# Moving the large SBUF buffers of a hybrid decoder step by 128 bytes

## The chip, the core and the metric

The kernel runs on one core of a Trainium2 chip, and all its work is in one launch. The metric is the device time in microseconds (us). TensorE (PE) multiplies matrices, and PEld is the part of it that loads weights; VectorE (DVE), ScalarE (ACT) and GpSimd (POOL) do elementwise work; SyncE (SP) issues DMAs. SBUF is the working memory that all of them read, 128 partitions side by side; every buffer begins at the same byte in each partition. TensorE writes to PSUM.

## The reference, cut to what matters

One inference step of a two-layer decoder on 576 tokens: 512 of a prompt and 64 of eight decoding sequences. The model is 1024 wide, and everything is float32.

```
for layer l in 0, 1:
    x += 0.5 * FFN_a(RMSNorm(x))      # silu(x @ w_gate) * (x @ w_up) @ w_down, inner width 2816
    x += Mixer_l(RMSNorm(x))          # layer 0: mLSTM matrix memory; layer 1: gated linear attention
    x += 0.5 * FFN_b(RMSNorm(x))
out = RMSNorm(x)
```

Outputs are the normed activations of all tokens, the new mixer states, normalisers, running maxima and the last convolution rows.

## The kernel before

Activations stay in SBUF with features on the partitions: `x` is 128 partitions x 8 tiles x 576 tokens. Each product of two float32 matrices is made from three products of `float32r` parts (`split_product`): high weight by high activation, high weight by low activation, low weight by high activation. So there are two buffers for each operand: `xn_hi` and `xn_lo` (normed activations), `w_hi` and `w_lo` (weights), `h_hi` and `h_lo` (the FFN's inner tiles), `th_hi` and `th_lo` (sums of activation tiles, for the blocks that `seven_pair` makes with seven products in place of eight).

A weight block is loaded by DMA into one of four slots of `raw`, 4096 bytes in each partition. ScalarE rounds it into `w_hi` (line 1185), VectorE writes what is left into `w_lo` (line 1753), and TensorE then multiplies with it. SyncE issues the load of a block once the block four places earlier has been split (lines 350 and 357), so that loads run ahead of the products.

The program goes through phases: for each FFN, three groups of a gate-and-up phase (G) and a down phase (D); for each mixer, QK, MIX and OUT. The first G of every FFN, the mixers and the very last D are written out in a straight line; other G and D phases are hardware loops. The plain products all stand on line 479, in `split_product`: tokens are cut in two halves of 288, and two matmuls with the same weights and the two halves follow one another (columns 0 to 287, then 288 to 575), into two PSUM banks. Those of `seven_pair` stand on line 536; line 753 makes the value tiles, with activations as weights. Lines 608, 784 and 787 are small products inside the mixers. Other names below: `gate_hi` and `gate_lo` are the few weight columns of the mixers' gates, read in slices that begin 144 bytes apart in mixer 0; `state` is the running prompt state of a mixer; `scratch` is ten tiles of 576 tokens for intermediate values; `n_in` is the incoming normaliser of the decoding sequences, 32 numbers (128 bytes) in each partition, read twice for each head in the mLSTM mixer (lines 2335 and 2339).

Buffers are laid out in the order of their declarations, each behind the one before. Where a name is closed again (`inner.close()`), the next declaration takes its place.

Of the kernel before, what the change touches and what calls it, by code (L numbers as in the profile page):

```python
# [7 lines left out]
SEQ, DEC_BATCH, DEC_SEQ = 512, 8, 8  # L8
N_HEADS, DK, DV = 4, 128, 256
# [5 lines left out]
P = 128  # L15
# [87 lines left out]
def program(nc, io):  # L103
# [4 lines left out]
    with ctx:  # L108
        def sb(name, shape, dt=f32):
            return ctx.enter_context(nc.sbuf_tensor(name, shape, dt))  # L110
# [2 lines left out]
            return ctx.enter_context(nc.semaphore(name))  # L113


        x = sb("x", [P, KT_X, TOK])

        inner = ExitStack()
# [33 lines left out]
        cols = sb("cols", [P, TT, 2 * N_HEADS])  # L152
        w_a2 = sb("w_a2", [GATE_RANK, N_HEADS * DK])
        b_a = sb("b_a", [P, N_HEADS])
        n_in = sb("n_in", [P, N_HEADS, DEC_BATCH])
        n_out = sb("n_out", [P, N_HEADS, DEC_BATCH + 1])
        n_state = sb("n_state", [P, N_CH])
        neg_b_a = sb("neg_b_a", [P, N_HEADS])
# [2568 lines left out]
```

How the kernel before makes its waits and increments, by code:

```python
            def load_mix(pair, mixer, first):  # L345
                for blk in range(2):
                    s = 2 * (pair % 2) + blk
                    sp.wait_ge(lo_done, 2 * pair + blk - 3)
                    sp.dma_start(raw[:, s, :], io["w_mix"][32 * mixer + first + blk, :, :]).then_inc(raw_full[s], 16)
# [1 line left out]
            def load(ph, i, s, first=False):  # L352
                n = 2 * ph["base"] + 4 * i + s
                if not first:
                    sp.wait_ge(lo_done, n - 3)
                sp.dma_start(raw[:, s, 0:ph["k"] * P],
                             block_source(ph, i, s).rearrange("o p n -> p (o n)")).then_inc(raw_full[s], 16)
# [1 line left out]
            def state_load(mixer, h):  # L360
                src, u = io["state_c"] if mixer == 0 else io["state_g"], N_HEADS * mixer + h
                if u:
                    sp.wait_ge(state_out, 32 * u)
                sp.dma_start(state_s[:, :, :], src[:, h, :, :].rearrange("b k v -> k b v")).then_inc(state_in, 16)
# [1 line left out]
            def state_store(mixer, h):  # L368
                dst_s, dst_p = (io["c_s"], io["c_p"]) if mixer == 0 else (io["s_s"], io["s_p"])
                sp.wait_ge(state_ready, N_HEADS * mixer + h + 1)
                sp.dma_start(dst_s[:, h, :, :].rearrange("b k v -> k b v"), state_s[:, :, :]).then_inc(state_out, 16)
                sp.dma_start(dst_p[h, :, :], state[:, N_CH - 1, :]).then_inc(state_out, 16)
# [196 lines left out]
            def token_sums(norm):  # L570
                pe.wait_ge(ssq_done, 4 * (norm + 1))
                if norm == 0:
```

## Time and profile before

| what | value |
|---|---|
| median of 3 runs | 2197.02 us (2196.39 to 2197.16) |
| profiled execution, first to last instruction | 2198.8 us |
| TensorE busy | 2160.5 us, 98% |
| VectorE busy | 1555.5 us, 71% |
| ScalarE busy | 951.1 us, 43% |
| GpSimd busy | 45.7 us, 2% |
| mean granted TensorE clock | 0.994 |
| moved by DMA | 201.58 MB, 92 GB/s |

The profiled execution is one run taken by the hardware profiler; its span is 1.8 us above the median of the runs that were only timed. The busy time of TensorE counts the stretch in which at least one matmul is under way. Matmuls overlap, so that "98% busy" says only that it had no gaps; how fast it goes is read from how many matmuls start in a stretch.

### The profile page before, as it was taken

The page shows a single profiled execution, that of the slowest core. Times are in us where ns is not written, and L with a number is a line of the kernel's source. Part 1 is how long each engine was busy: PE and PEld are TensorE (multiplying, and loading weights), DVE is VectorE, ACT ScalarE, POOL GpSimd, SP SyncE. Part 2 cuts the span into 40 slices and gives each one's busy share as a digit, 9 for nine tenths or more (in the row PEclk, how much of TensorE's full clock was granted, in tenths as well). Part 3 has the DMA queues.
Part 4 walks back from the last instruction along what each step waited for, and adds up shares of the span by engine and source line. Part 5 has one row for each costly group of instructions (what it writes and reads, how often), then busy time and mean ns, then how long its engine had stood idle before and what let it go on. Part 6 is the DMA issues. An engine that isn't in the chain of part 4 may idle for free.

```text
span 2198.8 us, 40702 instructions
## 1 busy us (share of the span) xinstructions
PE 2160.5 (98%) x16360; PEld 2137.4 (97%) x16360; DVE 1555.5 (71%) x2379; ACT 951.1 (43%) x1495; POOL 45.7 (2%) x50
## 2 busy tenths in 40 slices
PE   7999999999999999999999999999999999999997
PEld 7999999999999999999999999999999899999997
DVE  6898657685555798848679984863776457988485
ACT  5435435454433444515445452544322434445252
POOL 0000000001100000000000000000011100000000
PEclk9999999999999999999999999999999999999999
DMA  5222322224332232222323232232122222223222
GB/s 186 68 88 95 115 67 86 96 82 137 99 118 85 68 102 82 95 87 89 104 70 94 86 96 96 82 101 94 44 96 84 97 77 84 90 87 104 77 86 73
DMA packets 72578, 201.58 MB, mean 92 GB/s; under 512 B 7268, under 2 KB 26980, under 8 KB 72448
## 3 DMA queue, kind: packets, MB, share of 16 engines
q1 hardware_dynamic: 72448, 199.80, 28.1%
q8 instruction: 88, 1.44, 0.3%
q14 instruction: 42, 0.34, 0.1%
HBM read 187.82 MB, written 11.95 MB: 91 GB/s over the span
## 4 chain that ended last, share of the span: by engine, by line
PE 91%; DVE 5%; ACT 2%; issue 1%; DMA 0%; POOL 0%; SPq 0%; DVEq 0%; POOLq 0%
PE ps L479 48%; PE ps L536 32%; PE ps L753 4%; PE ps L608 1%; DVE w_lo L1768 1%; PE ps L784 1%; PE ps L773 1%; PE ps L787 0%; DVE w_lo L1753 0%; PE ps L803 0%; PE ps L617 0%; PE ps L796 0%; PE ps L631 0%; PE ps L797 0%; DMA x<-in_x 0%
## 5 line engine op out<-in xcount | busy, mean ns | idle before, releaser
L479 PE MATMUL ps<-h_lo,w_hi 128*128 128x288 f32 x1616 | 347.0, 294 | 4.1 <-DVE h_hi L2267 4.1
L479 PE MATMUL ps<-h_hi,w_hi 128*128 128x288 f32 x1616 | 346.5, 294 | 0.7 <-DVE w_lo L1753 0.7
L536 PE MATMUL ps<-th_hi,w_hi 128*128 128x288 f32 x1088 | 320.2, 294 | 2.4 <-ACT scratch L1219 2.4
L536 PE MATMUL ps<-th_lo,w_hi 128*128 128x288 f32 x1088 | 320.9, 295 | 0.0
L536 PE MATMUL ps<-th_hi,w_lo 128*128 128x288 f32 x1088 | 319.8, 294 | 0.0
L479 PE MATMUL ps<-h_hi,w_lo 128*128 128x288 f32 x1360 | 290.2, 292 | 0.0
L479 PE MATMUL ps<-xn_hi,w_hi 128*128 128x288 f32 x1152 | 257.2, 300 | 11.6 <-DVE w_lo L1753 8.9
L479 PEld LDWEIGHTS ps<-h_lo,w_hi 128*128 128x128 f32 x1616 | 259.9, 188 | 4.8 <-DVE h_hi L2267 4.5
L479 PEld LDWEIGHTS ps<-h_hi,w_hi 128*128 128x128 f32 x1616 | 259.9, 188 | 1.0 <-DVE w_lo L1753 0.9
L1753 DVE TENSOR_TENSOR w_lo<-raw,w_hi 128x1024 fp32r<-128x1024 f32 x196 | 232.2, 1221 | 36.9 <-ACT w_hi L1185 35.1
L479 PE MATMUL ps<-xn_hi,w_lo 128*128 128x288 f32 x1152 | 251.9, 296 | 0.0
L479 PE MATMUL ps<-xn_lo,w_hi 128*128 128x288 f32 x1152 | 251.7, 296 | 0.0
L1768 DVE TENSOR_TENSOR w_lo<-scratch,w_hi 128x512 fp32r<-128x512 f32 x272 | 181.8, 690 | 84.8 <-ACT w_hi L1200 84.4
L1185 ACT ACTIVATE w_hi<-raw 128x1024 fp32r<-128x1024 f32 x196 | 195.8, 1047 | 105.2 <-PE ps L479 80.5
L536 PE MATMUL ps<-xn_hi,w_lo 128*128 128x288 f32 x816 | 240.4, 295 | 0.0
L536 PE MATMUL ps<-xn_hi,w_hi 128*128 128x288 f32 x816 | 239.9, 294 | 0.0
L536 PE MATMUL ps<-xn_lo,w_hi 128*128 128x288 f32 x816 | 239.9, 294 | 0.0
L479 PEld LDWEIGHTS ps<-h_hi,w_lo 128*128 128x128 f32 x1360 | 217.5, 187 | 0.0
L536 PEld LDWEIGHTS ps<-th_hi,w_hi 128*128 128x128 f32 x1088 | 204.8, 188 | 3.7 <-issue 3.2
L479 PEld LDWEIGHTS ps<-xn_hi,w_hi 128*128 128x128 f32 x1152 | 187.7, 190 | 19.9 <-issue 17.5
L2019 DVE SCALAR_TENSOR_TENSOR x<-ps,x 128x1152 f32<-128x1152 f32 x52 | 70.5, 1356 | 191.9 <-PE ps L479 191.9
L536 PEld LDWEIGHTS ps<-th_hi,w_lo 128*128 128x128 f32 x1088 | 204.4, 188 | 0.0
(288 smaller groups left out, 4119.7 us busy)
## 6 DMA issues: line engine op xcount, KB each, us to landing
raw<-in_w_gate SPq DMA_DIRECT2D x88, 512.0 KB, 3.4
raw<-in_w_up SPq DMA_DIRECT2D x88, 512.0 KB, 4.2
raw<-in_w_down SPq DMA_DIRECT2D x64, 512.0 KB, 3.6
raw<-in_w_mix SPq DMA_DIRECT2D x64, 512.0 KB, 4.2
raw<-in_w_down SPq DMA_DIRECT2D x32, 384.0 KB, 3.2
state_s<-in_state_c SPq DMA_DIRECT2D x4, 1024.0 KB, 7.5
out_c_s<-state_s SPq DMA_DIRECT2D x4, 1024.0 KB, 4.6
state_s<-in_state_g SPq DMA_DIRECT2D x4, 1024.0 KB, 6.1
```

What stands on the lines that cost most here:

```text
L479: ins = nc.tensor.matmul(o, a, b[:, c] if c is not None else b, start=first and j == 0, stop=last and j == 2)
L536: ins = nc.tensor.matmul(ps[:, bank, FIRST], left, b_, start=first and k == 0 and j == 0, stop=k == KT_X // 2 - 1 and j == 2, skip_group_c ...
L608: ins = nc.tensor.matmul(ps[:, bank, c * P:(c + 1) * P], left[:, ts], right[:, ts], start=True, stop=True)
L753: ins = nc.tensor.matmul(out, a[:, k, xs], b[:, 2 * half:2 * half + 2, ws], start=k == 0 and j == 0, stop=k == KT_X - 1 and j == 2)
L773: ins = nc.tensor.matmul(ps[:, 4 + c // 2, (c % 2) * DV:(c % 2 + 1) * DV], k_tok[:, c, :], v_tok[:, 1 + c, h * DV:(h + 1) * DV], start=Tru ...
L784: ins = nc.tensor.matmul(out, v_tok[:, 1 + c, vs], att(mixer, h)[:, c * P:(c + 1) * P], start=True, stop=c == 0)
L1185: nc.scalar.activation(w_hi[:, slot, :], raw[:, slot, :], ACT.Copy).then_inc(hi_done, 1)
L1753: V.tensor_tensor(w_lo[:, slot, :], raw[:, slot, :], w_hi[:, slot, :].bitcast(f32), ALU.subtract).then_inc(lo_done, 1)
L1768: return V.tensor_tensor(by_tile(unit(w_lo, half, u)), src, by_tile(unit(w_hi, half, u)).bitcast(f32), ALU.subtract)
L2019: ins = V.scalar_tensor_tensor(xs, ps[:, b:b + 4, 0:HALF_TOK], scale, xs, ALU.mult, ALU.add)
```

## The change

The declaration of `n_in` moves from behind `b_a` to the front, ahead of `x`.

```diff
@@ -113,6 +113,7 @@
             return ctx.enter_context(nc.semaphore(name))


+        n_in = sb("n_in", [P, N_HEADS, DEC_BATCH])
         x = sb("x", [P, KT_X, TOK])

         inner = ExitStack()
@@ -152,7 +153,6 @@
         cols = sb("cols", [P, TT, 2 * N_HEADS])
         w_a2 = sb("w_a2", [GATE_RANK, N_HEADS * DK])
         b_a = sb("b_a", [P, N_HEADS])
-        n_in = sb("n_in", [P, N_HEADS, DEC_BATCH])
         n_out = sb("n_out", [P, N_HEADS, DEC_BATCH + 1])
```

On every engine the same instructions stand in the same order as before; only addresses in them differ. The first byte of each buffer in a partition, as the two programs are built:

| buffer | size | before | after | before mod 256 | after mod 256 |
|---|---|---|---|---|---|
| `n_in` | 128 | 207264 | 1152 | 160 | 128 |
| `x` | 18432 | 1152 | 1280 | 128 | 0 |
| `xn_hi` | 18432 | 19584 | 19712 | 128 | 0 |
| `xn_lo` | 18432 | 38016 | 38144 | 128 | 0 |
| `raw` | 16384 | 56448 | 56576 | 128 | 0 |
| `w_hi` | 16384 | 72832 | 72960 | 128 | 0 |
| `w_lo` | 16384 | 89216 | 89344 | 128 | 0 |
| `h_hi` (also `qt`, `kt`) | 18432 | 105600 | 105728 | 128 | 0 |
| `h_lo` (also `og`) | 18432 | 124032 | 124160 | 128 | 0 |
| `th_hi` (also `v_tok`) | 18432 | 142464 | 142592 | 128 | 0 |
| `scratch` | 23040 | 162944 | 163072 | 128 | 0 |
| `cst` | 4384 | 188608 | 188736 | 192 | 64 |
| `gate_hi` | 2112 | 196064 | 196192 | 224 | 96 |
| `gate_lo` | 2112 | 198176 | 198304 | 32 | 160 |
| `th_lo` (also `state`, `state_s`) | 18432 | 207808 | 207808 | 192 | 192 |

All that is declared between `x` and `b_a` moves by 128 bytes; `n_out` and what follows it stay.

## Rows read from the trace of the kernel before

**Rows 1.** The page: busy time, granted clock in 40 slices, and the chain by line.
```profile
PE 2160.5 (98%) x16360; PEld 2137.4 (97%) x16360; DVE 1555.5 (71%) x2379; ACT 951.1 (43%) x1495; POOL 45.7 (2%) x50
...
PEclk9999999999999999999999999999999999999999
...
PE ps L479 48%; PE ps L536 32%; PE ps L753 4%; PE ps L608 1%; DVE w_lo L1768 1%; PE ps L784 1%; PE ps L773 1%; PE ps L787 0%; DVE w_lo L1753 0%; PE ps L803 0%; PE ps L617 0%; PE ps L796 0%; PE ps L631 0%; PE ps L797 0%; DMA x<-in_x 0%
```

**Rows 2.** Waits of TensorE, longest in total first: us, times, longest.
```profile
PE ps L479 <- DVE w_lo L1753: 9.5, 2, 8.9
PE ps L479 <- DVE h_hi L2267: 4.1, 2, 2.1
PE ps L1118 <- DVE scratch L2588: 3.7, 1, 3.7
PE ps L536 <- ACT scratch L1219: 2.4, 4, 0.7
```

**Rows 3.** Busy time by stretch, instructions as (x), clock, DMA; G, G, D, QK, OUT, seven.
```profile
48.00:80.00 32.00, 32.00 (x243) 32.00 (x242) 21.23 (x32) 10.63 (x14) 0.00 (x0) 1.00 0.21 67
728.00:760.00 32.00, 32.00 (x248) 32.00 (x247) 22.55 (x32) 11.96 (x15) 0.00 (x0) 1.00 0.20 66
800.00:832.00 32.00, 32.00 (x248) 32.00 (x247) 30.94 (x33) 12.98 (x13) 0.00 (x0) 1.00 0.23 78
432.00:464.00 32.00, 32.00 (x242) 32.00 (x242) 29.36 (x64) 19.88 (x31) 0.24 (x2) 1.00 0.22 67
664.00:696.00 32.00, 32.00 (x242) 32.00 (x241) 15.44 (x14) 10.16 (x12) 0.00 (x0) 1.00 0.30 96
200.00:232.00 32.00, 32.00 (x244) 32.00 (x244) 27.77 (x50) 18.89 (x39) 0.00 (x0) 1.00 0.25 83
```

**Rows 4.** Groups of matmuls by line and form: count, busy us, mean ns.
```profile
L479 PE MATMUL ps<-h_lo,w_hi 128*128 128x288 f32 x1616 | 347.0, 294 | 4.1 <-DVE h_hi L2267 4.1
L536 PE MATMUL ps<-th_lo,w_hi 128*128 128x288 f32 x1088 | 320.9, 295 | 0.0
L536 PE MATMUL ps<-th_hi,w_lo 128*128 128x288 f32 x1088 | 319.8, 294 | 0.0
```

**Rows 5.** TensorE in order of time, from the first gate matmul to the one after.
```profile
413.81 0.43 PE L479 MATMUL ps<-xn_hi,gate_hi 128*128 128x288 f32 x2
...
420.19 0.30 PE L479 MATMUL ps<-xn_hi,w_hi 128*128 128x288 f32 x1
```

**Rows 6.** TensorE in order of time in the mLSTM mixer: start us, us.
```profile
500.70 0.61 PE L784 MATMUL ps<-scratch,v_tok 128*128 128x128 f32 x4
501.15 0.39 PE L787 MATMUL ps<-qt,state 128*128 128x128 f32 x2
501.37 0.39 PE L784 MATMUL ps<-scratch,v_tok 128*128 128x128 f32 x2
```

**Rows 7.** All engines in order of time, start of the program.
```profile
8.86 0.82 PE L479 MATMUL ps<-xn_hi,w_hi 128*128 128x288 f32 x2 [8.86 <-DVE w_lo L1753]
```

**Rows 8.** Waits of ScalarE for DMAs.
```profile
ACT xn_hi L1274 <- DMA x<-in_x: 3.2, 2, 2.9
ACT w_hi L1185 <- DMA raw<-in_w_up: 0.2, 1, 0.2
ACT gate_hi L1694 <- DMA n_in<-in_n_in: 0.2, 1, 0.2
```

**Rows 9.** Weight loads: KB each and median us to landing; then SyncE's waits.
```profile
raw<-in_w_gate SPq DMA_DIRECT2D x88, 512.0 KB, 3.4
raw<-in_w_up SPq DMA_DIRECT2D x88, 512.0 KB, 4.2
...
SPq L357 <- DVE w_lo L1768: 817.5, 136, 18.2
```

**Rows 10.** Busy time by stretch: start, and the tail behind the last FFN matmul.
```profile
0.00:9.00 9.00, 0.14 (x1) 0.18 (x2) 2.94 (x4) 4.93 (x6) 0.52 (x5) 1.00 0.76 283
...
2184.60:2198.80 14.20, 1.33 (x2) 0.50 (x2) 8.77 (x16) 1.13 (x2) 0.00 (x0) 0.63 0.41 142
```

## The prediction

> **What bounds the kernel now.** I read the page first, then the waits of TensorE, then stretches of 32 us inside single phases. The page has TensorE busy for 2160.5 of 2198.8 us at a granted clock of nine tenths or more in all 40 slices (full speed, 2.4 GHz), and the chain that ended last is TensorE's, 48% on line 479 and 32% on line 536 [rows 1]. Its waits are few: the largest are 9.5 us for a weight split, nearly all at the start, 4.1, 3.7 and 2.4 us [rows 2]. So the time is, to within some 40 us, the number of matmuls times the pace at which they start.
>
> That pace is the one thing that a new address could move by much, so I read it closely. A matmul of 288 columns shows a duration of 294 ns [rows 4], but they overlap; a window of 32 us counts every one that touches it, so the pace is (32.00 + 0.29) us over the count. It is 132.9 ns in the G phase at 48 us and 130.2 ns in the G phase at 728 us; the D loop at 800 us has 130.2, the QK phase at 432 us and the OUT phase at 664 us have 133.4, and the seven-product loop at 200 us has 132.3 [rows 3]. The two G stretches are the same lines with the same buffers at the same addresses, and still differ by 2.7 ns. The pace of line 479 thus has two levels, and which one holds is not fixed by the addresses alone.
>
> **The change part by part.** No instruction is added, removed or moved. All costs are therefore differences in how long the same instruction takes, or the same transfer.
>
> *Moving operands of the matmuls.* An activation tile of `xn_*`, `h_*` or `th_*` is read in halves of 1152 bytes = 9 x 128. The 16 halves of a buffer therefore begin at all 16 multiples of 128 within 2048 bytes, each once. A shift by 128 only permutes that set. Whatever a start costs by its place within 256, 512, 1024 or 2048 bytes, the sum over a buffer is the same: 0 us. The one operand that does not move is `th_lo`, at 192 mod 256 beside `th_hi` at 128: its halves start at odd multiples of 64, the others' at multiples of 128. Its matmuls show 295 ns, those of `th_hi` 294 [rows 4], and the loop that uses both goes at 132.3 ns, between the two paces of the loops that never touch it [rows 3]. The place of that operand costs nothing that I can see.
>
> *Weights.* This is the only real novelty. Weight tiles are 512 bytes, so all of `w_hi` and `w_lo` begin at 128 mod 512 before and at 256 mod 512 after. Nearest rows: the gate weights, whose slices begin 144 bytes apart from 224 mod 256 (every place in steps of 16 bytes, 0 mod 256 among them). Their 48 matmuls take 420.19 - 413.81 = 6.38 us, 132.9 ns each, which is not above the 133.4 of ordinary weights in the same phase [rows 5, 3]. Short matmuls of 128 columns, where the weight load must show, start every 0.11 us with weights of `v_tok` (128 mod 256: 0.45 us for four) as with weights of `state` (192 mod 256: 0.22 us for two) [rows 6]. The three kinds agree within 0.5 ns for the long form. I take 0. The ends: 0.5 ns either way on the 15,200 long matmuls of lines 479, 536 and 753 (16360 in all less about 1,100 short ones) is 7.6 us either way; that is the resolution of these rows, not a sign of an effect.
>
> *Relative places.* A weight load runs under the previous matmul, so two reads of SBUF meet. Between weights and moving operands all distances stay as they were, except to `th_lo` and `state`. Cost 0, by the same rows.
>
> *VectorE and ScalarE.* They have slack: VectorE is busy 71%, ScalarE 43% [rows 1]. If all their instructions took 1% more, only where TensorE waits for them would it show: 1% of the roughly 20 us of waits in [rows 2] and of the 14.2 us tail, where VectorE is busy 8.77 us [rows 10]: 0.3 us. I take 0, ends -0.3 and +0.3.
>
> *DMAs.* Loads of weights land 3.4 to 4.2 us after issue, while SyncE has waited 817.5 us in total for slots to come free [rows 9]: the queue, not the transfer, sets when they arrive, and ScalarE waited for a weight load once, 0.2 us [rows 8]. Even a load that takes a tenth longer is covered. Only the start is bare: the first matmul begins at 8.86 us [rows 7], and before it ScalarE waits 3.2 us in total for `x` [rows 8] while the DMA engines are 76% busy [rows 10]. A transfer that gets 5% shorter or longer there is worth 5% of 9 us, 0.45 us. I take -0.1.
>
> Here the Trainium skill has a rule that speaks for a gain ("DMA: Bandwidth & Descriptors", section "How a descriptor splits into AXI transactions"): a transaction must start at a multiple of 256 bytes, and a descriptor that doesn't start there also pays for the bytes below it. If it holds for the SBUF side of a load, a row of 4096 bytes at 128 mod 256 costs 132 beats of 32 bytes before and 128 after, an estimate of 3% from that page. By it the start would gain about 0.3 us and the rest nothing, since loads are hidden; no row here shows a transfer at 0 mod 256 to compare.
>
> *`n_in` itself.* It is loaded last of the constants, one transfer of 16 KB, and ScalarE waits 0.2 us once for that group [rows 8]. VectorE reads it in eight short instructions in the mixer. 0 us.
>
> The sum: 0 + 0 + 0 + 0 - 0.1 + 0 = -0.1 us on a span of 2198.8, so 2198.7 in a profiled execution. The profiled span is 1.8 us above the timed median, so against the median of 2197.02 the forecast is 2196.9, which I give as 2197.0. What can be told from no change here is about 0.2%, 4.4 us: everything in the sum is far inside it.
>
> **The rivals.**
>
> *A, faster: the pace of the straight-line phases locks at the lower level.* The straight-line matmuls of line 479 that now run at 133.3 ns are at most 480 in the first G phase, 1536 in the two mixers and 768 in the two OUT phases, 2784. If the new addresses brought them all to 130.0, the gain is 2784 x 3.3 ns = 9.2 us: 2187.8. For it: the same code with the same operands runs at either pace [rows 3], so something slight decides, and it may be the history of the run, in which addresses could play a part. Against it: three timed runs lie within 0.8 us, so that the timing noise of a run doesn't flip the levels, and all distances between operands stay.
>
> *B, slower: the loops lock at the upper level.* The D loops now run at 130.2 ns [rows 3]. They issue 22 tiles x 8 blocks x 6 matmuls for each of 4 FFNs, less the last D phase of 288, so 3936. At 133.3 ns they cost 3936 x 3.3 ns = 13.0 us more: 2210. If only a third of them flipped, it would be +4.3 us, the point from which the verdict is slower. The place where it would decide is the weight load of line 479 at its new start, 256 mod 512, under a moving read. For it: the same as for A, and no steady loop of before has had weights there. Against it: the gate weights, at 16-byte steps, are no slower than the rest [rows 5].
>
> *C: the address matters in the weights of every long matmul by one more or one less step of access.* Bounded above at 0.5 ns either way, 7.6 us: 2189.4 or 2204.6. Against it stands that three kinds of weights agree. The Trainium skill ("SBUF — State Buffer", section "Specifications (TRN2)") counts lines of 16 bytes; every start of a large buffer is a multiple of 16 before and after, so by that page the sum stays 0.
>
> *D: the change is only in the DMAs.* That gives at most 0.45 us, within the forecast's own range.
>
> **How the numbers follow.** No measurable change (the sum, with D): 0.77. A, or the faster half of C: 0.12. B, or the slower half of C: 0.11. The likeliest one's own range is 2195.3 to 2198.7: the spread of the runs before (0.8 us) doubled, plus 0.8 us for DMAs and side engines. The two sides together hold 0.23, more than may be left out, so the range reaches half of A (2192.4) and the lower third of B (2201.3): 2192.0 to 2201.0. The chances of faster by over 0.2%, within it, and slower by over it are 0.12, 0.77 and 0.11.
>
> **What would show it.** If I am right, a window of 32 us holds 242 or 243 matmuls at 48, 432 and 664 us, 248 at 728 and 800 us, and 244 at 200 us, as now; the waits of TensorE stay near 9.5, 4.1, 3.7 and 2.4 us; the first matmul starts at 8.4 to 9.3 us. A shows as 248 in the windows of QK and OUT, B as 242 in the D loops, C as a count that is shifted in all windows at once. The landing time of weight loads tells of the DMA rule: 3.4 us would fall to 3.3 with no effect on TensorE. The prediction is wrong if the time leaves 2192.6 to 2201.4.

## The result, and the profile after

The changed kernel takes 2214.16 us (median of 4 runs, 2211.35 to 2216.96) against 2197.09 us (4 runs): a ratio of 1.0075, 95% interval 1.0061 to 1.0089. It is 17 us slower. The forecast was 2197.0 us, no measurable change. The interval leaves room for a difference of 13.4 to 19.6 us. The profiled executions last 2198.8 us before and 2210.4 us after.

The page of the changed kernel, its busy time, answers to [rows 1]:

```profile
span 2210.4 us, 40702 instructions
...
PE 2171.0 (98%) x16360; PEld 2148.1 (97%) x16360; DVE 1554.1 (70%) x2379; ACT 949.3 (43%) x1495; POOL 47.5 (2%) x50
```

The same instructions; VectorE and ScalarE are as busy as before to within 2 us, and TensorE is busy 10.5 us longer. TensorE's waits answer to [rows 2] and have hardly moved:

```profile
PE ps L479 <- DVE w_lo L1753: 10.1, 2, 9.4
PE ps L479 <- DVE h_hi L2267: 4.1, 2, 2.1
PE ps L1118 <- DVE scratch L2588: 3.7, 1, 3.7
PE ps L536 <- ACT scratch L1219: 2.3, 4, 0.7
```

So it is the pace of the matmuls. The changed kernel by stretch, in the order of [rows 3] (G, G, D, QK, OUT, seven-product loop), the columns as there; after the second PE column stands the number of matmuls:

```profile
48.00:80.00 32.00, 32.00 (x242) 32.00 (x241) 22.75 (x33) 11.03 (x14) 0.00 (x0) 1.00 0.20 67
728.00:760.00 32.00, 32.00 (x249) 32.00 (x248) 21.70 (x29) 13.12 (x17) 0.00 (x0) 1.00 0.24 82
800.00:832.00 32.00, 32.00 (x242) 32.00 (x241) 30.39 (x34) 14.09 (x14) 0.00 (x0) 1.00 0.28 93
432.00:464.00 32.00, 32.00 (x242) 32.00 (x241) 30.73 (x63) 20.15 (x30) 0.23 (x2) 1.00 0.20 67
664.00:696.00 32.00, 32.00 (x242) 32.00 (x241) 16.85 (x16) 12.19 (x14) 0.00 (x0) 1.00 0.25 84
200.00:232.00 32.00, 32.00 (x243) 32.00 (x243) 27.60 (x49) 18.52 (x38) 0.00 (x0) 1.00 0.24 85
```

Five of the six are as before, to one or two matmuls. The D loop at 800 us has 242 where it had 248: (32.00 + 0.29) / 242 = 133.4 ns a matmul, in place of 130.2. It is no exception: the windows of 32 us at 120, 264, 936, 1056, 1200 and 1904 us hold 242 or 243 each, where before they held 248 or 249. The window of 80 us in a seven-product loop is long enough to show the smaller step there. The kernel before, then the changed one:

```profile
170.00:250.00 80.00, 80.00 (x607) 80.00 (x607) 68.21 (x120) 45.09 (x93) 0.00 (x0) 1.00 0.30 97
```

```profile
170.00:250.00 80.00, 80.00 (x604) 80.00 (x603) 68.19 (x121) 45.11 (x93) 0.00 (x0) 1.00 0.28 94
```

That is 80.29 us over 607, 132.3 ns, against 132.9. By kind of operand, the groups of the changed kernel that answer to [rows 4] (count, busy us, mean ns):

```profile
L479 PE MATMUL ps<-h_lo,w_hi 128*128 128x288 f32 x1616 | 350.7, 296 | 4.1 <-DVE h_hi L2267 4.1
L536 PE MATMUL ps<-th_hi,w_hi 128*128 128x288 f32 x1088 | 324.1, 298 | 2.3 <-ACT scratch L1219 2.3
L536 PE MATMUL ps<-th_lo,w_hi 128*128 128x288 f32 x1088 | 322.3, 296 | 0.0
```

The `th` matmuls have grown; those of `th_hi` with `w_hi` took 320.2 us at a mean of 294 ns before. The `xn` matmuls of the same line stay at 294 ns. From one start to the next on line 536 the `th` ones now take 133.3 ns and the `xn` ones 132.3, before 132.1 and 132.3 (starts in the trace, averaged by operand; how the places where the operand changes are counted moves them by 0.1).

**The account.** By the starts in the trace all 11 D loops run at 130.0 ns before and at 133.3 after: 3936 matmuls x 3.33 ns = 13.1 us. The `th` matmuls: 3264 x 1.2 ns = 3.9 us. Three straight-line stretches that stand directly behind a D loop have slowed with it, 0.6 us in all. The clearest is a G phase of 96 matmuls, from 130.0 to 133.3 ns, before and then after:

```profile
1090.00:1101.00 11.00, 11.00 (x87) 11.00 (x86) 8.56 (x12) 7.39 (x9) 0.00 (x0) 1.00 0.34 114
```

```profile
1096.00:1107.00 11.00, 11.00 (x85) 11.00 (x84) 8.58 (x11) 6.98 (x9) 0.00 (x0) 1.00 0.31 103
```

Together 17.6 us, beside a timed difference of 17.1 that is known to 3 us either way. The profiled executions differ by only 11.6 us, since they did not have the same clock. Stretches around the places where the kernel before was profiled with TensorE's clock at half (1.2 GHz in place of 2.4) for a moment, before and then at the same places of the changed kernel, the last two of which come 10 or 11 us later:

```profile
40.00:44.00 4.00, 3.19 (x15) 3.23 (x16) 3.84 (x5) 1.08 (x2) 0.00 (x0) 0.66 0.54 155
652.00:662.00 10.00, 7.94 (x49) 7.74 (x48) 5.59 (x11) 1.41 (x3) 0.00 (x0) 0.83 0.41 133
1632.00:1642.00 10.00, 7.79 (x53) 7.62 (x52) 9.09 (x16) 3.70 (x5) 3.36 (x4) 0.83 0.00 0
1745.00:1755.00 10.00, 7.94 (x50) 7.74 (x49) 5.85 (x10) 1.24 (x2) 0.00 (x0) 0.83 0.43 151
```

```profile
40.00:44.00 4.00, 2.65 (x20) 2.69 (x21) 3.82 (x5) 1.62 (x2) 0.00 (x0) 1.00 0.37 123
652.00:662.00 10.00, 7.94 (x62) 7.74 (x61) 6.45 (x12) 2.29 (x3) 0.00 (x0) 1.00 0.24 84
1643.00:1653.00 10.00, 7.80 (x65) 7.57 (x64) 9.10 (x19) 4.74 (x6) 5.10 (x4) 1.00 0.00 0
1755.00:1765.00 10.00, 7.94 (x61) 7.73 (x60) 7.06 (x12) 2.68 (x4) 0.00 (x0) 1.00 0.40 135
```

A mean clock of 0.83 over 10 us is 3.4 us at half speed, a loss of 1.7 us; 0.66 over 4 us, with 0.91 in the next 4, is the same again. In three of these stretches TensorE had been idle for 2 us at the edge of a phase (busy 7.94 or 7.79 of 10 us), and ahead of the one at 41 us for 1.9 us. The changed kernel has the same idle times (busy 7.94, 7.80 and 7.94) and kept its full clock, so the idle time alone does not decide. The profile before has these four and one at 475 us, the profile after only the last: 4 x 1.7 = 6.8 us. 17.6 - 6.8 = 10.8 us, and the first matmul starts 0.56 us later (9.42 us, against [rows 7]); that leaves 0.2 us. The four timed runs of the changed kernel differ by 5.6 us, and their mean granted clocks go with their times: 0.997 and 0.996 in the two of 2211 and 2212 us, 0.995 and 0.994 in those of 2216 and 2217.

### The profile page after: what moved, and what is told of

It is laid out like the page before. It is cut to its first block, busy times and chain, and to the rows that moved or that the text cites. A ratio compares the mean times of both kernels' runs of the same rounds, so it can differ in the third digit from the quotient of the medians.

```text
span 2210.4 us, 40702 instructions
## 1 busy us (share of the span) xinstructions
PE 2171.0 (98%) x16360; PEld 2148.1 (97%) x16360; DVE 1554.1 (70%) x2379; ACT 949.3 (43%) x1495; POOL 47.5 (2%) x50
## 4 chain that ended last, share of the span: by engine, by line
PE 91%; DVE 5%; ACT 2%; issue 1%; DMA 0%; POOL 0%; SPq 0%; DVEq 0%; POOLq 0%
PE ps L479 48%; PE ps L536 32%; PE ps L753 4%; PE ps L608 1%; DVE w_lo L1768 1%; PE ps L784 1%; PE ps L773 1%; PE ps L787 0%; DVE w_lo L1753 0%; PE ps L803 0%; PE ps L617 0%; DMA x<-in_x 0%; PE ps L631 0%; PE ps L796 0%; PE ps L797 0%
## 5 line engine op out<-in xcount | busy, mean ns | idle before, releaser
L479 PE MATMUL ps<-h_hi,w_lo 128*128 128x288 f32 x1360 | 295.1, 296 | 0.0
```

The costliest lines, as they stand in the source:

```text
L479: ins = nc.tensor.matmul(o, a, b[:, c] if c is not None else b, start=first and j == 0, stop=last and j == 2)
```

## The experiments

All of them keep every instruction of the kernel before, except where it says that a matmul is added. The changes are places in memory. Unless a ratio is given, a time is of one execution, beside one of the kernel before. Those of the kernel before took 2194.1 to 2200.9 us, so a difference of a few us in one pair says little, and the paces decide. In each fence the rows are windows with the columns of [rows 3]: 170 us is in a seven-product loop, 264 and 800 us are in D loops, 728 us in a G phase. Before, they held 607, 249, 248 and 248 matmuls.

**1. The 128 bytes ahead of `h_hi`.** Weights, `x` and `xn` stay.

```diff
-        n_in = sb("n_in", ...)            # behind b_a
+        n_in = sb("n_in", ...)            # ahead of h_hi
```

> The 128 bytes stand ahead of h_hi: weights, raw, x and xn stay where they were before; h_hi, h_lo, th_hi, scratch and all behind them begin 128 bytes later. If the start of the weight tiles sets the pace of the D loops (theory 1), they stay at 130.0 ns a matmul, 248 in the window of 32 us at 800 us, and the time at 2197 us or, with the 0.7 ns more in the seven-product loops, up to 2201. If the start of the moving tiles h sets it (theory 2), 242 in that window and about 2212. If the history at the entry of a loop sets it (theory 3), either pace, unlike the place of any buffer.

2216.56 us, beside 2199.39. Its windows at 170 and 800 us:

```profile
170.00:250.00 80.00, 80.00 (x605) 80.00 (x604) 68.25 (x121) 45.06 (x93) 0.00 (x0) 1.00 0.29 93
800.00:832.00 32.00, 32.00 (x242) 32.00 (x242) 30.40 (x36) 12.94 (x13) 0.00 (x0) 1.00 0.30 99
```

The loss is all there with the weights unmoved. Theory 1, which was also the mechanism of rival B, is out.

**2. Ahead of `w_hi`.** `x`, `xn` and `raw` stay.

```diff
+        n_in = sb("n_in", ...)            # ahead of w_hi
```

> The 128 bytes stand ahead of w_hi: raw, x and xn stay, w_hi, w_lo and all behind them begin 128 bytes later. Theory 1 (weights): D loops at 133.3 ns, 242 in 32 us, about 2212 us. Theory 2 (h): the same. Theory 4 (raw and x begin at a multiple of 256 bytes, and the transfers into them disturb the reads of TensorE): 130.0 ns, 248, 2197 us.

2211.37 us, beside 2199.39. Its windows at 728, 170 and 800 us:

```profile
728.00:760.00 32.00, 32.00 (x243) 32.00 (x242) 22.12 (x31) 10.86 (x14) 0.00 (x0) 1.00 0.21 66
170.00:250.00 80.00, 80.00 (x603) 80.00 (x602) 67.73 (x120) 43.62 (x91) 0.00 (x0) 1.00 0.30 98
800.00:832.00 32.00, 32.00 (x242) 32.00 (x242) 31.32 (x34) 12.52 (x12) 0.00 (x0) 1.00 0.23 76
```

Theory 4 (transfers) is out, since neither `raw` nor `x` moved. New is the G phase at 728 us: 243, where the changed kernel has 249. Here the distance of `w_*` to `xn_*` has changed, in the change it has not. The D loop at 120 us held 249 and that at 1904 us 248: not all D loops fell.

**3. All by 256 bytes.**

```diff
+        n_in = sb("n_in", ...); head_w = ...; b_a = ...; m_in = ...     # 256 bytes, ahead of x
```

> Four small buffers of 256 bytes in all stand ahead of x: all large buffers are at 128 mod 256 again, as before, but at 384 mod 512. If a rule of 256 bytes sets the pace: 130.0 ns in the D loops, 2197 us. If one of 512 bytes or more, another value than before is to be expected, 133.3 ns and about 2212 us. By theory 3 (history) it could be either.

2197.78 us, beside 2199.39. Its windows at 170 and 800 us:

```profile
170.00:250.00 80.00, 80.00 (x607) 80.00 (x606) 67.99 (x120) 44.38 (x93) 0.00 (x0) 1.00 0.31 98
800.00:832.00 32.00, 32.00 (x249) 32.00 (x248) 31.32 (x34) 11.98 (x12) 0.00 (x0) 1.00 0.23 73
```

As before in both, and in every other window read. A shift of all but `th_lo` by 256 bytes does nothing where one by 128 costs 17 us, so places seem to count modulo 256.

**4. Ahead of `th_hi`.** D loops read nothing that moved.

```diff
+        n_in = sb("n_in", ...)            # ahead of th_hi
```

> The 128 bytes stand ahead of th_hi: th_hi, v_tok, scratch and all up to b_a begin 128 bytes later; x, xn, raw, weights and h stay. D loops read nothing that moved: by theories 1, 2 and 4 they stay at 130.0 ns (248 in 32 us). The seven-product loops, which go from 132.1 to 132.8 ns with the change, do so here if the distance of th_hi to th_lo is the cause (4 us), and stay if weights are. By theory 3 the D loops could fall to 133.3 ns, since what they follow changed its pace.

2204.56 us, beside 2199.39. Its windows at 170, 264 and 800 us:

```profile
170.00:250.00 80.00, 80.00 (x605) 80.00 (x604) 68.13 (x121) 45.13 (x94) 0.00 (x0) 1.00 0.29 92
264.00:296.00 32.00, 32.00 (x248) 32.00 (x248) 10.37 (x11) 5.17 (x6) 0.00 (x0) 1.00 0.23 74
800.00:832.00 32.00, 32.00 (x242) 32.00 (x241) 30.50 (x33) 13.39 (x13) 0.00 (x0) 1.00 0.23 81
```

The seven-product loop slowed, as `th_hi` alone had moved in it. And of the D loops, those at 120, 800 and 1200 us fell to 242, while those at 264, 936, 1056 and 1904 us stayed at 248. All read the same buffers, which had not moved. So the pace of a D loop is not a matter of its own addresses alone. One rival is left here: the three that fell are first D loops of an FFN, during which VectorE and ScalarE write `th_*`, as they do also in the one at 1904 us, which did not fall. Run 6 answers it.

**5. The change, with `th_lo` moved too.**

```diff
+        n_in = sb("n_in", ...)            # ahead of x
+        inner.enter_context(nc.sbuf_tensor("gap", [P, 32], f32))        # 128 bytes ahead of th_lo
```

> The change, and th_lo 128 bytes later as well: every operand of the long matmuls has moved by 128 bytes. Theory R: what counts is the distance mod 256 between the buffers that one loop reads; in the change only the distance to th_lo differs, it slows the seven-product loops (132.1 to 133.2 ns where th is read), and the D loops behind them fall to 133.3 ns through the state in which they are entered. By R this kernel is back at 130.0 ns in the D loops (248 in 32 us at 800 us) and 132.1 in the seven-product loops: 2197 to 2199 us. Theory Z (an absolute place, weights or h at 0 mod 256 are slow): D loops stay at 133.3, 2208 to 2214 us.

2200.65 us, beside 2194.14; one execution of each, timed again below. Its windows at 170 and 800 us:

```profile
170.00:250.00 80.00, 80.00 (x607) 80.00 (x606) 68.45 (x121) 45.23 (x93) 0.00 (x0) 1.00 0.29 96
800.00:832.00 32.00, 32.00 (x248) 32.00 (x247) 30.39 (x34) 13.94 (x14) 0.00 (x0) 1.00 0.27 91
```

`w_*`, `h_*` and `xn_*` stand exactly where they do in the changed kernel, and the D loops are back at 248. What differs is `th_lo`, which no D loop reads.

**6. `th_lo` alone by 128 bytes.**

```diff
+        inner.enter_context(nc.sbuf_tensor("gap", [P, 32], f32))        # ahead of th_lo
```

> The kernel before with th_lo alone 128 bytes later; D loops and G products read nothing that moved. Theory R: the distance to th_lo is that of the change, so th matmuls of line 536 at 133.2 ns and some or all D loops at 133.3: 2202 to 2214 us. Theory Z: 2197 us with D loops at 130.0.

2214.42 us, beside 2194.14. Its windows at 170 and 800 us:

```profile
170.00:250.00 80.00, 80.00 (x605) 80.00 (x604) 68.22 (x120) 44.71 (x93) 0.00 (x0) 1.00 0.29 96
800.00:832.00 32.00, 32.00 (x242) 32.00 (x241) 30.39 (x36) 13.77 (x14) 0.00 (x0) 1.00 0.31 98
```

The loss of the change without its move. Common to both are only the distances from the other buffers to `th_lo`, with `th_hi` 64 mod 256 before and 192 in the change; run 4, which moved `th_hi`, and run 7 show that it is the one to `th_hi` which slows the `th` matmuls. All 11 D loops run at 133.3 ns here by their starts. During those at 264, 936 and 1056 us no engine reads or writes `th_*`, so it is not the writes, and their code and all that they read stand as in the kernel before. So their pace comes from what ran before them.

**7. The weights alone, mod 256.**

```diff
+        n_in = sb("n_in", ...)            # ahead of w_hi
+        head_w = ...; b_a = ...; m_in = ...                             # 128 bytes more, ahead of h_hi
```

> w_hi and w_lo 128 bytes later, everything from h_hi to b_a 256 bytes later, x, xn and raw unmoved: mod 256 the weights alone have moved. Theory R: all pairs with weights are off by 128: D loops at 133.3 ns, the G windows at 728 and 1120 us at 242 or 243 in place of 248, both kinds of line 536 slower: 2211 us or more. Theory Z for weights: as R. Theory Z for h, or for what VectorE and ScalarE write: 2197 us.

2213.32 us, beside 2194.14. Its windows at 728, 170 and 800 us:

```profile
728.00:760.00 32.00, 32.00 (x242) 32.00 (x241) 21.05 (x30) 12.93 (x17) 0.00 (x0) 1.00 0.24 84
170.00:250.00 80.00, 80.00 (x607) 80.00 (x606) 68.16 (x120) 45.56 (x94) 0.00 (x0) 1.00 0.29 92
800.00:832.00 32.00, 32.00 (x243) 32.00 (x242) 30.39 (x36) 13.93 (x14) 0.00 (x0) 1.00 0.30 97
```

The G phase fell to 242 and the D loops too. But the seven-product loop kept 607, against what R said: its `th` matmuls stayed at 132.2 ns, its `xn` matmuls went to 132.9. For `th` the distance to the weights does not count, only that between `th_hi` and `th_lo`; for `xn` that to the weights does. R holds for some pairs and not for all.

**8. `scratch` and what lies behind it.**

```diff
+        n_in = sb("n_in", ...)            # ahead of scratch
```

> Only scratch and what lies behind it up to b_a is 128 bytes later: no operand of a long matmul has moved, but nearly all that VectorE and ScalarE read and write beside them has. Theories R and Z: 2197 to 2199 us, D loops at 130.0 ns. If the traffic of the other engines sets the pace: some D loops at 133.3, up to 2212 us.

2197.58 us, beside 2194.14, and all paces as before (608 and 248). So where VectorE and ScalarE read and write their intermediate values beside TensorE is not the cause.

**9. One small matmul ahead of each D loop.** First in the kernel before, then in the changed one.

```diff
+        pe.wait_ge(psum_free, ...)                         # the wait with which the loop itself begins
+        matmul(ps[:, 0, 488:492], ones, ones[:, 0:4])      # float32, once ahead of each of 11 D loops
```

> The kernel before with the same added matmul ahead of each of the 11 D loops. Theory H: the D loops may stay at 130.0 ns or some go to 133.3, up to 2212 us. Theory A: all stay at 130.0, 2196 to 2199 us.

> The changed kernel, with one added matmul of 4 float32 columns between the phase before and each of the 11 D loops; nothing reads its result and no address differs from the change. If the pace of a D loop is a state that it takes over at its entry (theory H), some of the D loops that stand at 133.3 ns go to 130.0 (248 in 32 us): down to 2201 us if all do. If the pace is a property of the addresses in the loop (theory A): all 11 stay at 133.3, 2212 to 2217 us.

The kernel before with it: 2213.78 us, beside 2198.74. Its windows at 170, 264 and 800 us:

```profile
170.00:250.00 80.00, 80.00 (x608) 80.00 (x607) 68.51 (x121) 45.42 (x94) 0.00 (x0) 1.00 0.29 92
264.00:296.00 32.00, 32.00 (x242) 32.00 (x241) 8.78 (x8) 5.18 (x6) 0.00 (x0) 1.00 0.24 79
800.00:832.00 32.00, 32.00 (x243) 32.00 (x242) 30.43 (x36) 12.32 (x13) 0.00 (x0) 1.00 0.31 99
```

No buffer has moved, the seven-product loop still has 608, and the D loops are at 242. The 11 matmuls of 4 columns cost 0.2 us each at their place (starts in the trace), 2.2 us; the pace of the loops behind them costs 13.1, together 15.3 us beside a measured 15.0. The changed kernel with it: 2217.49 us, and its D loops stay at 243 and 242.

Taken alone, this run has a rival: the added instructions also shift TensorE's code behind them. Runs 4 and 6 have no such shift, and D loops fall in them too. A straight-line stretch shows it too. The G phase of 96 matmuls at some 1090 us follows directly on a D loop, reads only weights and `xn_*`, and takes over that loop's pace. Runs 4, 6 and 9 (the kernel before), whose D loop ahead of it ran at 130.0, 133.3 and 133.3 ns:

```profile
1092.00:1103.00 11.00, 11.00 (x87) 11.00 (x87) 8.63 (x11) 6.93 (x9) 0.00 (x0) 1.00 0.35 121
```

```profile
1097.00:1108.00 11.00, 11.00 (x85) 11.00 (x84) 8.59 (x11) 6.97 (x9) 0.00 (x0) 1.00 0.29 102
```

```profile
1099.00:1110.00 11.00, 11.00 (x85) 11.00 (x84) 8.57 (x12) 7.44 (x9) 0.00 (x0) 1.00 0.31 109
```

In the 18 profiles in which weights and `xn_*` keep their distance, this stretch runs at 130.0 ns in the 6 where the D loop ahead does, and at 133.2 to 133.4 in the 12 where it does not. So theory H holds for the loss: a D loop has two paces, and which one it gets depends on what ran ahead of it.

**10. Other distances of `th_lo`.** A gap of 192, 64, 32 or 224 bytes ahead of it, in the kernel before.

> The kernel before with th_lo 192 bytes later, at 128 mod 256 like th_hi: the distance is 0, as it always is for xn_hi and xn_lo, whose matmuls in the same loops take 132.3 ns. By theory R with distance as the only thing: th matmuls of line 536 at about 132.3 (64 gave 132.1, 192 gave 133.3), and the D loops by the state they take over, 2197 or 2210 us. If a distance of 64 is needed, 133.3 and 2210.

> The kernel before with th_lo 64 bytes later, at 0 mod 256: a distance of 128 to th_hi. Theory R gives no value beforehand; between 132.1 and 133.3 ns for the th matmuls if distance acts smoothly, below 132.1 if 128 is the best one. D loops at 130.0 or 133.3. 2195 to 2214 us.

> The kernel before with th_lo 32 bytes later: 96 bytes mod 256 from th_hi (64 before: th matmuls of line 536 at 132.1 ns; 128: 133.0; 0 and 192: 133.3). If distance acts smoothly: between 132.1 and 133.0. If only 64 is good: 133.0 to 133.3. D loops at 130.0 only if the loop ahead of them ends as it does before.

> The kernel before with th_lo 224 bytes later: 32 bytes mod 256 from th_hi. Smooth: between 132.1 (64) and 133.3 (0). Only 64 good: 133.3. D loops 130.0 or 133.3 by how the loop ahead ends, 2197 to 2216 us.

Distances 0, 128, 96 and 32 in this order, one fence for each kernel: the window at 170 us, and for the first also that at 800 us.

```profile
170.00:250.00 80.00, 80.00 (x604) 80.00 (x604) 68.21 (x121) 45.08 (x93) 0.00 (x0) 1.00 0.29 93
800.00:832.00 32.00, 32.00 (x242) 32.00 (x241) 30.51 (x33) 13.39 (x13) 0.00 (x0) 1.00 0.26 83
```

```profile
170.00:250.00 80.00, 80.00 (x605) 80.00 (x605) 68.44 (x121) 44.76 (x92) 0.00 (x0) 1.00 0.29 92
```

```profile
170.00:250.00 80.00, 80.00 (x607) 80.00 (x606) 68.21 (x120) 44.88 (x93) 0.00 (x0) 1.00 0.31 97
```

```profile
170.00:250.00 80.00, 80.00 (x606) 80.00 (x605) 68.15 (x120) 45.36 (x94) 0.00 (x0) 1.00 0.28 92
```

| distance mod 256 | `th` matmul, ns | D loops | us |
|---|---|---|---|
| 64 (before) | 132.1 | 130.0 | 2197 |
| 96 | 132.5 | 133.3 | 2211.87 |
| 32 | 132.9 | 133.3 | 2212.71 |
| 128 | 133.0 | 133.3 | 2217.92 |
| 0 | 133.3 | 133.3 | 2210.92 |
| 192 (changed) | 133.3 | 133.3 | 2214.16 |

(Starts in the trace, averaged; the kernel before ran in 2197.37 to 2198.74 beside them.) The pace of the `th` matmuls goes up in steps on both sides of 64, not by one rule of distance for all buffers: `h_hi` and `h_lo` lie at a distance of 0 in every kernel here, and their loops ran at 130.0 and at 133.3 ns. The D loops show no steps: of the six distances, with nothing but `th_lo` moved, only 64 leads into them so that they run at 130.0 ns.

**11. Two of them timed.** The kernels of 5 and 6 again.

> The change with th_lo 128 bytes later too, timed. Theory R with H (the distance of th_hi to th_lo sets the pace of the seven-product loops and, through their end, the state of the D loops): a ratio of 1.000 to the kernel before, within 0.2%. If another part of the change costs as well, 1.001 to 1.003, since one look gave 2200.65 beside 2194.14.

> The kernel before with th_lo alone 128 bytes later, timed. By R with H it is the whole of what the change costs: a ratio of 1.0075, as the change has, within 1.006 to 1.009. If the moved weights, h and xn carry part of it, less than 1.005.

The change with `th_lo` moved along: 2198.39 us, ratio 1.0001 (0.9991 to 1.0010). `th_lo` alone: 2214.07 us, ratio 1.0072 (1.0055 to 1.0089). The first is no measurable change, the second as much as the change, 1.0075. Both were profiled again, and all 11 D loops had the paces of 5 and 6, 130.0 and 133.3 ns.

**12. Two other matmuls ahead of the D loops of the changed kernel.**

```diff
+        matmul(ps[:, 0, 288:480], ones, cst[:, 0:192])                    # first kernel, float32
+        matmul(ps[:, 0, 0:288], gate_hi[:, 0:128], gate_hi[:, 0:288])     # second kernel, float32r
```

> The changed kernel with one added float32 matmul of 192 columns ahead of each of the 11 D loops (some 0.4 us each, 4.6 us in all), as the token sums have, behind which straight-line G products were seen to go from 133.3 to 130.0 ns. Theory H: D loops at 130.0 ns again at the addresses of the change, 2214 - 13 + 5 = 2206 us, if this seam leads into the fast state; 2218 if not. Theory A (addresses in the loop): 133.3 in all, 2218 us.

> The changed kernel with one added float32r matmul of 288 columns (gate weights, result overwritten) ahead of each of the 11 D loops, 0.13 us each. Theory H: the loop is entered in another state, and some D loops may go to 130.0 ns: down to 2202 us if all do. Theory A: 133.3 in all 11 and 2215 us.

Both have the wait of run 9 as well, the second also one for `gate_lo`. 2217.47 and 2217.74 us, beside 2200.90; the D loops at 800 us:

```profile
800.00:832.00 32.00, 32.00 (x242) 32.00 (x241) 30.39 (x37) 12.45 (x13) 0.00 (x0) 1.00 0.32 99
```

```profile
800.00:832.00 32.00, 32.00 (x243) 32.00 (x242) 30.39 (x35) 13.57 (x14) 0.00 (x0) 1.00 0.31 99
```

Neither led back to 130.0 ns, and the hope of 2206 and of 2202 us in the expectations was not met. Inconclusive for H: that the fast pace can be reached in all D loops with a distance of 192 has not been shown. In runs 2 and 4, also at 192, two and eight of the 11 D loops did run at 130.0 ns. No kernel here was shown to be faster than the one before.

## Why the prediction was wrong

*What bounds the kernel* was right: no wait, transfer or other engine moved the time, and the pace of the matmuls is what did.

*The step that failed* is the one on relative places: "all distances stay as they were, except to `th_lo` and `state`. Cost 0, by the same rows". It named the exception and gave it no price, and it weighed weights against moving operands, not the two moving operands `th_hi` and `th_lo` against each other. The rows showed the pace at a distance of 64; they could say nothing of 192. I compared `th_lo`'s matmuls with `th_hi`'s at one layout, saw 295 and 294 ns, and took it that the place costs nothing, where both belong to a pair and share its pace. The distances to `th_lo` were the only ones between operands of the long matmuls that the change altered, and that was plain in the table of addresses. By run 6 the one from `th_hi` is worth 3.9 us directly and sends the D loops from 130.0 to 133.3 ns, 13.1 us; of that way, through the loop in front, the prediction had nothing.

*The moving operands*: that a shift only permutes the starts of the 16 halves is borne out by run 5, where all have moved and the time is the same. *Weights*: cost 0 was right for the shift itself (5), though not for a shift of the weights against `xn` (7). The row behind it was read too widely: slices 144 bytes apart, from 224 in `gate_hi` and from 32 in `gate_lo`, begin at 12 of the 16 places in steps of 16 bytes, not at every one. *VectorE, ScalarE, DMAs*: their 0.3 and 0.1 us could not be seen; the median landing times of the loads of `w_gate` and `w_up` went from 3.4 and 4.2 us to 3.4 and 4.0. Over all profiles those of `w_up` are 3.6 to 4.2 us with `raw` at 128 mod 256 and 3.7 to 4.1 with it at 0, and the first matmul begins at 8.9 to 10.0 us with `x` at 128 (14 profiles) and at 8.9 to 9.5 with it at 0 (6), with a mean of 9.3 us in both. So the 0.56 us of the changed kernel is scatter, and so is the gain of 0.3 us not seen. The Trainium skill's rule on 256-byte starts ("DMA: Bandwidth & Descriptors", section "How a descriptor splits into AXI transactions") gave that gain if it holds for the SBUF side of a load; these times show no such effect.

*Rival B* had the right place, the right pace and the right size (3936 x 3.3 ns, 2210 us), but not the right mechanism: it put the cause on the weights' start at 256 mod 512, and runs 1, 5 and 6 exclude that. Nor was its chance, 0.11, well argued. Against it I held that run-to-run noise doesn't flip the levels. That was no argument: executions of one program can enter a loop alike, as the two profiles each of 5 and 6 did, but the change alters the pace of the loop in front, and with it the way into all D loops at once. The rows of before held the warning: the same code at 132.9 and 130.2 ns [rows 3] meant that 3936 matmuls were running at the better of two paces for a reason that I could not name.

*Rival A*, the same effect the other way, was not seen in the changed kernel; in run 10 at distance 0 the G phase at 48 us holds 249, where before it held 243, so it exists. That stretch reads nothing that moved and lies ahead of the first seven products; what set its pace is not shown. *Rival C* (0.5 ns on every weight, 7.6 us) is excluded by the kernel of 5, timed within 2.2 us of the one before (11).

What stays open: what in the chip keeps the two paces, why the loops take over one of them, and whether an added instruction can bring the fast one about. For the change it is shown that the distance of `th_lo` to `th_hi` costs all of it, and that a D loop can fall through what runs ahead of it; which feature of the seven-product loop's end does it is not. Also whether the slow D loops of run 7 come from their own distance of weights to `h_*` or from the way in, and why in run 4 eight of the 11 D loops stayed at 130.0 ns and in run 6, with the same distance, none.

## What to carry to other kernels

When TensorE is the bound, read how many matmuls start in fixed windows of each phase, and compare phases with the same code: two paces for one code are a gain or a loss that any small edit may flip. When a change moves buffers, tabulate the distances modulo 256 bytes between all buffers that one loop reads, those that did not move first, and treat a changed distance as unknown in cost rather than as free. And a loop whose own operands are untouched can still change pace, if what runs ahead of it does.

## What the runs showed of the hardware

- Back-to-back float32r matmuls of 288 columns run at 130.0 or at 133.3 ns, with the same code and the same operands, and each of the 11 D loops stays at the one or the other over its whole length; one added matmul of 4 columns ahead of each took all 11 from the first to the second (9). The straight-line G phase at some 1090 us, directly behind a D loop, takes over its pace (4, 6, 9). The other direction was not reached by an added matmul (9, 12).
- In a loop that reads `th_hi` and `th_lo` in turn, the pace of their matmuls depends on the distance modulo 256 bytes: 132.1 ns at 64, 133.3 at 0 and 192 (10). A shift of all operands of the long matmuls by 128 bytes (5), or of all but `th_lo` by 256 (3), does nothing.
- The Trainium skill counts SBUF lines of 16 bytes ("SBUF — State Buffer", section "Specifications (TRN2)"), and by it none of these moves would matter, since all are multiples of 32. The measurement decides: at the six distances tried, the `th` matmuls go at 132.1 to 133.3 ns, 0.9% apart.
- TensorE's clock falls to half (1.2 GHz) for 3.4 us at a time, 1.7 us lost each. Ahead of the tail this came five times in the profile of the kernel before and once in that of the changed one. It goes with the spread of one kernel: in 13 timed runs of the kernel before beside run 11, the mean granted clock was 0.994 in the slowest (2200.5 us) and 0.996 in the fastest (2195.9).
